# Moving the dense operand tiles by 64 bytes and the experts' operand tiles by 64 bytes in a two-block transformer kernel

## The chip, the cores and the metric

The kernel runs on one core of one Trainium2 chip. The metric is the device time of one execution in microseconds. The kernel before takes 1743.59 us, the median of three runs (1742.76 to 1747.4).

## The reference, cut to what matters

256 tokens of width 1024 pass through two blocks, all in float32. The first has a gated convolution branch, an attention with latent queries and keys, and a feed-forward part with a short convolution. The second has a pooling and convolution mixer, a gated feed-forward part, a sliding-window attention, and a mixture of 8 experts with two experts for each token:

```python
def swiglu(h, w_gate, w_up, w_down):
    return (jax.nn.silu(h @ w_gate) * (h @ w_up)) @ w_down

def moe_swiglu(h, w_router, w_gate, w_up, w_down):      # 8 experts, hidden width 3584
    ...
    for e in range(N_EXPERTS):
        out = out + combine[..., e:e + 1] * swiglu(h, w_gate[e], w_up[e], w_down[e])
```

Every large product is `h @ w` with h of 256 rows, or the 128 gathered rows of one expert. The weights are read once from HBM, in some 450 pieces of 1 MB.

## The kernel before, in words

**Products in three parts.** A float32 product is made of three products in the type fp32r. Each weight and each operand is split into a high part (rounded to fp32r) and a low part (the rest). The helper `three` (lines 771 to 773) issues high times high, high times low and low times high into the same PSUM bank. A name such as `psum<-ah,whi` in the profile gives the output, then the operand that streams through TensorE (the moving operand, here `ah`), then the one that is loaded into it beforehand (the stationary operand, here a 128x128 piece of `whi`).

**Weights.** They arrive in granules of 128 x 2048 numbers (1 MB) in the six slots of `wraw`. ScalarE writes a granule's high part to `whi` (three slots), VectorE its low part to `wlo` (three slots): lines 1261 and 1593, and line 1660. The SP queue loads the next granule when VectorE is through with the slot. ScalarE's split waits until TensorE has used the slot of `whi` that it overwrites.

**Dense stages.** Here the weights are stationary, and an operand of 128 x 256 numbers moves; one granule holds 16 pieces and makes 48 matmuls. Which operand tiles move depends on the stage. `ah` and `al` (high and low, eight chunks of 256 columns) hold the normalised input: of the first projection, both up projections, the mixer's input and the second attention's queries, keys and values. `fh`/`fl` serve the two down projections, `mh`/`ml` the products `w_out` and `mix_out`, `oh`/`ol` and `lnh`/`lnl` the outputs of attention and of the convolution branch (`oh` in this profile stands for both attentions' tiles).

**Experts.** The loop runs over 8 experts with 42 granules each. Here the operand is stationary: a 128x128 piece of `xgh`/`xgl` (the gathered inputs) for the gate and up products, or of `ath`/`atl` (the activations) for the down product. 512 columns of `whi` or `wlo` move. Four transposes (line 1184) stand between groups of these.

**Placement.** The helper `place(name, shape, dtype, at)` puts a tile into SBUF. Without `at` tiles follow one another from the start address, each size rounded up to 64 bytes; with `at` a tile lies at that offset from the address `region`, which follows the last tile of the first kind. All tiles of the first kind before `ah` (`wraw`, `whi`, `wlo`) have sizes that are multiples of 8 KB. Call their start address B modulo 128. Then `ah` and `al` start at B too. After them come `xres` and `sq` (8 KB each), five tiles of 1 KB, `par` (496 numbers, 1984 bytes), `con` (rounded 1408), `ones` (512), `st` (128), `gfg` and `nsk` (64 each), `rgain` (256), `rtm` and `flag` (64 each). Of these only sizes that are odd multiples of 64 matter modulo 128: `par` (31 times 64) and the four of 64 bytes. So `region` starts at B + 64 modulo 128. The tiles `fh`, `fl`, `mh`, `ml`, `lnh`, `lnl`, `oh`, `ol`, `oh2`, `ol2` and, in the experts, `xgh`, `xgl`, `ath`, `atl` are all at multiples of 128 from `region`. So are `last`, `ylh` and `yll`, with which the last matmuls of the kernel (lines 1241 and 1242) pick out the last expert's rows: `last` is stationary, 512 columns of `ylh` or `yll` move, and these operands are fp32r too.

Of the kernel before, what the change touches and what calls it, by code (L numbers as in the profile page):

```python
# [15 lines left out]
P = 128  # L16
T = 256
D = 1024
KD = D // P
# [8 lines left out]
NE = 8  # L28
# [253 lines left out]
def program(nc, wall, x_d, params_d, consts_d, pos_d, onehot_d, relb_d, poolw_d, recip_d, fgain_d,  # L282
            mgain_d, scratch, rows_in, rows_out, out_d):
    f32, f32r, i32 = mybir.dt.float32, mybir.dt.float32r, mybir.dt.int32
# [4 lines left out]
    with ctx:  # L289
        top = [(nc.sbuf_base + 63) // 64 * 64]  # L290

        def place(name, shape, dt, at=None):

            size = (int(np.prod(shape[1:])) * 4 + 63) // 64 * 64
            off = top[0] if at is None else region + at
            if at is None:
                top[0] += size
            assert at is None or at + size <= region_size, name
            return nc.alloc_sbuf_tensor_at(name, shape, dt, offset=off)
# [5 lines left out]
        wraw = place("wraw", [P, NW, GW], f32)  # L305
        whi = place("whi", [P, NS, GW], f32r)
        wlo = place("wlo", [P, NS, GW], f32r)
        ah_at = top[0]
        ah = place("ah", [P, KD, T], f32r)
        al = place("al", [P, KD, T], f32r)  # L310
        xres = place("xres", [P, KD, T], f32)
# [8 lines left out]
        par = place("par", [P, NPARAM], f32)  # L320
        con = place("con", [P, NCONST], f32)
        ones = place("ones", [P, P], f32)
        st = place("st", [P, 2, 16], f32)
        gfg = place("gfg", [P, KD], f32)
        nsk = place("nsk", [P, NH2], f32)
        rgain = place("rgain", [P, KD, NE], f32)
        rtm = place("rtm", [P, 2], f32)
        flag = place("flag", [P, 1], i32)
        region = top[0]
        region_size = nc.sbuf_usable_end - 64 - region  # L330
        KB = 1024
# [62 lines left out]

        zeros = place("zeros", [P, D], f32, 20 * KB)

        xgh = place("xgh", [P, KD, P], f32r, 0)
        xgl = place("xgl", [P, KD, P], f32r, 4 * KB)
        ath = place("ath", [P, 2, 4, P], f32r, 8 * KB)
        atl = place("atl", [P, 2, 4, P], f32r, 12 * KB)  # L400
        htm = place("htm", [P, 2, D], f32, 16 * KB)
        xtm = place("xtm", [P, 2, D], f32, 24 * KB + 128)
        mgain = place("mgain", [P, D + P], f32, 64 * KB + 128)
        hrow = place("hrow", [P, 2, DW], f32, 56 * KB)
# [23 lines left out]
        xgt = place("xgt", [P, D], f32, 48 * KB)  # L428
        ysb = place("ysb", [P, D], f32, 52 * KB)
        yrow1 = place("yrow1", [P, 2, D], f32, 56 * KB)  # L430
        yrow2 = place("yrow2", [P, 2, D], f32, 16 * KB)
        outb = place("outb", [P, 2, D], f32, 0)
        ylh = place("ylh", [P, D], f32r, 48 * KB)
        yll = place("yll", [P, D], f32r, 8 * KB)
# [1973 lines left out]
```

## Time and profile before

| | us |
|---|---|
| median of the runs | 1743.59 |
| the profiled execution | 1746.71 |
| its span, first to last instruction | 1744.9 |
| granted TensorE clock, mean share of full speed | 0.991 |

The profiled execution is 3.1 us above the median and inside the range of the runs; 1.8 us of it lie outside the span. The experts' loop runs from about 768 to 1728 us of the span, the dense stages lie before it. In the profile, TensorE's matmul records overlap, since matmuls are pipelined: the start of one to the start of the next is the pace, while the duration of one is longer and has a modelled end. Weight loads are a row of their own (PEld).

### The profile page before, as it was taken

What the parts mean: (1) busy time and instruction counts of PE and PEld (TensorE: products, weight loads), DVE (VectorE), ACT (ScalarE), POOL (GpSimd) and SP (SyncE); (2) the same over time, 40 slices, a digit from 0 to 9 for tenths busy, and PEclk for the clock granted to TensorE, in tenths of its full rate; (3) what the DMA queues carried; (4) which work ended last, traced back from release to release, by engine and by line L of the source; (5) the groups of instructions that cost most, each with busy time, mean ns of one, the idle gap of its engine ahead of it and who ended that gap; (6) DMA issues with size and microseconds to landing.
All of it is one profiled execution on the core that took longest, in us unless ns stands there. A gap on an engine that the chain in (4) does not pass through costs nothing.

```text
span 1744.9 us, 26269 instructions
## 1 busy us (share of the span) xinstructions
PE 1709.2 (98%) x10136; PEld 1514.7 (87%) x10136; DVE 1418.2 (81%) x1392; ACT 1125.2 (64%) x1132; POOL 189.8 (11%) x167
## 2 busy tenths in 40 slices
PE   8999999999999999899999999999999999999997
PEld 8989999999999999887888888888888888888885
DVE  6996788857866657677888888888888888888888
ACT  5325577653544445566777777777777777777775
POOL 6000354412400011020000000000000000000200
PEclk9999999999999999999999999999999999999998
DMA  8335599894555555159999999999999999999993
GB/s 320 128 121 193 151 234 337 320 254 173 180 183 194 180 198 161 73 197 408 397 368 381 382 377 380 364 385 387 359 390 380 369 380 380 379 383 352 398 422 154
DMA packets 75614, 513.50 MB, mean 294 GB/s; under 512 B 8368, under 2 KB 8848, under 8 KB 17424
## 3 DMA queue, kind: packets, MB, share of 16 engines
q1 hardware_dynamic: 68832, 487.13, 73.9%
q0 software_dynamic: 6560, 25.31, 5.4%
q8 instruction: 52, 0.85, 0.2%
q14 instruction: 26, 0.21, 0.0%
q10 hardware_dynamic: 144, 0.00, 0.0%
HBM read 488.27 MB, written 24.14 MB: 294 GB/s over the span
## 4 chain that ended last, share of the span: by engine, by line
PE 86%; DVE 7%; ACT 2%; issue 1%; DMA 1%; POOL 1%; DVEq 0%; SPq 0%; POOLq 0%; ACTq 0%
PE psum L771 27%; PE psum L773 26%; PE psum L772 26%; PE psum L824 3%; DVE wlo L1660 2%; PE psum L1184 1%; DVE acc L1744 1%; DMA wraw<-weights 1%; ACT whi L1261 1%; PE psum L1049 0%; PE psum L1152 0%; PE psum L905 0%; PE psum L926 0%; ACT whi L1593 0%; DMA par<-params 0%
## 5 line engine op out<-in xcount | busy, mean ns | idle before, releaser
L1660 DVE TENSOR_TENSOR wlo<-wraw,whi 128x2048 fp32r<-128x2048 f32 x445 | 1014.5, 2280 | 198.8 <-ACT whi L1593 115.6
L1593 ACT ACTIVATE whi<-wraw 128x2048 fp32r<-128x2048 f32 x336 | 644.6, 1919 | 234.2 <-PE psum L773 225.5
L771 PE MATMUL psum<-whi,xgh 128*128 128x512 f32 x896 | 357.8, 399 | 2.9 <-DVE wlo L1660 2.0
L773 PE MATMUL psum<-whi,xgl 128*128 128x512 f32 x896 | 351.1, 392 | 0.0
L772 PE MATMUL psum<-wlo,xgh 128*128 128x512 f32 x896 | 350.0, 391 | 0.0
L771 PE MATMUL psum<-ah,whi 128*128 128x256 f32 x1048 | 299.9, 286 | 4.4 <-DVE u L1750 3.9
L772 PE MATMUL psum<-al,whi 128*128 128x256 f32 x1048 | 297.2, 284 | 0.0
L773 PE MATMUL psum<-ah,wlo 128*128 128x256 f32 x1048 | 297.1, 284 | 0.0
L1261 ACT ACTIVATE whi<-wraw 128x2048 fp32r<-128x2048 f32 x104 | 198.5, 1910 | 123.5 <-PE psum L773 119.6
L771 PEld LDWEIGHTS psum<-ah,whi 128*128 128x128 f32 x1048 | 201.7, 192 | 5.9 <-DVE u L1750 4.5
L773 PEld LDWEIGHTS psum<-whi,xgl 128*128 128x128 f32 x896 | 168.6, 188 | 39.3
L772 PEld LDWEIGHTS psum<-al,whi 128*128 128x128 f32 x1048 | 201.8, 193 | 0.3
L773 PEld LDWEIGHTS psum<-ah,wlo 128*128 128x128 f32 x1048 | 201.8, 193 | 0.0
L771 PEld LDWEIGHTS psum<-whi,xgh 128*128 128x128 f32 x896 | 168.8, 188 | 37.2 <-DVE wlo L1660 2.4
L772 PEld LDWEIGHTS psum<-wlo,xgh 128*128 128x128 f32 x896 | 168.9, 188 | 34.7
L771 PE MATMUL psum<-whi,ath 128*128 128x512 f32 x448 | 177.8, 397 | 0.0
L773 PE MATMUL psum<-whi,atl 128*128 128x512 f32 x448 | 175.3, 391 | 0.0
L772 PE MATMUL psum<-wlo,ath 128*128 128x512 f32 x448 | 174.7, 390 | 0.0
L755 POOL DMA_INDIRECT yrow<-expert_outs,idx x4 | 9.6, 2398 | 867.2 <-SPq L560 866.3
L773 PEld LDWEIGHTS psum<-whi,atl 128*128 128x128 f32 x448 | 84.1, 188 | 19.5
L772 PEld LDWEIGHTS psum<-wlo,ath 128*128 128x128 f32 x448 | 84.2, 188 | 17.6
L771 PEld LDWEIGHTS psum<-whi,ath 128*128 128x128 f32 x448 | 84.2, 188 | 17.3 <-DVE wlo L1660 0.3
(349 smaller groups left out, 2234.6 us busy)
## 6 DMA issues: line engine op xcount, KB each, us to landing
wraw<-weights SPq DMA_DIRECT2D x453, 1024.0 KB, 5.1
expert_rows<-zeros POOLq DMA_DIRECT2D x1, 8704.0 KB
expert_outs<-zeros POOLq DMA_DIRECT2D x1, 4608.0 KB
expert_outs<-ysb SPq DMA_DIRECT2D x8, 512.0 KB, 6.5
xgt<-expert_rows SPq DMA_DIRECT2D x8, 512.0 KB, 6.0
bias_rows<-ttab POOLq DMA_DIRECT2D x1, 3072.0 KB, 37.2
btab<-bias_rows POOLq DMA_DIRECT2D x4, 384.0 KB, 8.1
xres<-x SPq DMA_DIRECT2D x1, 1024.0 KB, 5.0
```

The costliest lines, as they stand in the source:

```text
L755: pool.indirect_dma_start(out=dst[:, t, :], out_offset=None, in_=rows_out, in_offset=bass.IndirectOffsetOnAxis(ap=idx[:, i:i + 1], axis=0) ...
L771: nc.tensor.matmul(out, lh, rh, start=start, stop=False)
L772: nc.tensor.matmul(out, lh, rl, start=False, stop=False)
L773: return nc.tensor.matmul(out, ll, rh, start=False, stop=stop)
L824: mm = nc.tensor.matmul(jb(n), wraw[:, g % NW, off:off + P], x[:, k, :], start=(k == 0), stop=(k == PLAN.jobs[n][-1][2]))
L1184: mm = nc.tensor.transpose(bank[6][:, i * P:(i + 1) * P], act_[:, i * P:(i + 1) * P], ident)
L1261: sc.activation(whi[:, i % NS, :], wraw[:, g % NW, :], ACT.Copy).then_inc(hi_done, 1)
L1593: sc.activation(whi[:, (GS + j) % NS, :], wraw[:, g % NW, :], ACT.Copy).then_inc(hi_done, 1)
L1660: return ve.tensor_tensor(dst, value, hi.bitcast(f32), SUB)
L1744: ve.scalar_tensor_tensor(acc[:, c, :], u[:, c, tap:tap + T], pcol("conv_dw_w", 4 * tap + c), acc[:, c, :], MUL, ADD).then_inc(conv_step, 1)
```

## The change

Three small tiles are placed ahead of `ah` where before they came after `ones`. They take 128 + 256 + 64 = 448 bytes, so `ah`, `al`, and all from there to `ones` start 448 bytes later, which is 64 bytes modulo 128. The sum of all sizes is the same, so `region` does not move. Five tiles of the experts' part, and `yrow2`, get 64 bytes more in their offset from `region`. No instruction is added, removed or put in another place.

Modulo 128, before: `ah`/`al` at B as the weights, `xgh`/`xgl`/`ath`/`atl` at B + 64. After: `ah`/`al` at B + 64, `xgh`/`xgl`/`ath`/`atl` at B as the weights. All others named above stay at B + 64. `xres`, `sq`, `rstd` and their like move with `ah` to B + 64.

```diff
         wlo = place("wlo", [P, NS, GW], f32r)
-        ah_at = top[0]
+        st = place("st", [P, 2, 16], f32)
+        rgain = place("rgain", [P, KD, NE], f32)
+        flag = place("flag", [P, 1], i32)
         ah = place("ah", [P, KD, T], f32r)
         al = place("al", [P, KD, T], f32r)
...
         ones = place("ones", [P, P], f32)
-        st = place("st", [P, 2, 16], f32)
         gfg = place("gfg", [P, KD], f32)
         nsk = place("nsk", [P, NH2], f32)
-        rgain = place("rgain", [P, KD, NE], f32)
         rtm = place("rtm", [P, 2], f32)
-        flag = place("flag", [P, 1], i32)
...
-        xgh = place("xgh", [P, KD, P], f32r, 0)
-        xgl = place("xgl", [P, KD, P], f32r, 4 * KB)
-        ath = place("ath", [P, 2, 4, P], f32r, 8 * KB)
-        atl = place("atl", [P, 2, 4, P], f32r, 12 * KB)
-        htm = place("htm", [P, 2, D], f32, 16 * KB)
+        xgh = place("xgh", [P, KD, P], f32r, 64)
+        xgl = place("xgl", [P, KD, P], f32r, 4 * KB + 64)
+        ath = place("ath", [P, 2, 4, P], f32r, 8 * KB + 64)
+        atl = place("atl", [P, 2, 4, P], f32r, 12 * KB + 64)
+        htm = place("htm", [P, 2, D], f32, 16 * KB + 64)
...
-        yrow2 = place("yrow2", [P, 2, D], f32, 16 * KB)
+        yrow2 = place("yrow2", [P, 2, D], f32, 16 * KB + 64)
```

## Rows read from the trace of the kernel before

**Rows 1.** The page: busy time by engine, and the chain that ended last, by line.

```profile
PE 1709.2 (98%) x10136; PEld 1514.7 (87%) x10136; DVE 1418.2 (81%) x1392; ACT 1125.2 (64%) x1132; POOL 189.8 (11%) x167
...
PE psum L771 27%; PE psum L773 26%; PE psum L772 26%; PE psum L824 3%; DVE wlo L1660 2%; PE psum L1184 1%; DVE acc L1744 1%; DMA wraw<-weights 1%; ACT whi L1261 1%; PE psum L1049 0%; PE psum L1152 0%; PE psum L905 0%; PE psum L926 0%; ACT whi L1593 0%; DMA par<-params 0%
```

**Rows 2.** The page's costliest groups: busy us, mean ns of one, idle before.

```profile
L1660 DVE TENSOR_TENSOR wlo<-wraw,whi 128x2048 fp32r<-128x2048 f32 x445 | 1014.5, 2280 | 198.8 <-ACT whi L1593 115.6
L771 PE MATMUL psum<-whi,xgh 128*128 128x512 f32 x896 | 357.8, 399 | 2.9 <-DVE wlo L1660 2.0
L771 PE MATMUL psum<-ah,whi 128*128 128x256 f32 x1048 | 299.9, 286 | 4.4 <-DVE u L1750 3.9
L773 PEld LDWEIGHTS psum<-ah,wlo 128*128 128x128 f32 x1048 | 201.8, 193 | 0.0
L771 PE MATMUL psum<-whi,ath 128*128 128x512 f32 x448 | 177.8, 397 | 0.0
```

**Rows 3.** Line 771's matmuls counted in stretches of stages in which `ah` moves.

```profile
219.00:330.00 111.00, 87.04 (x308) 1.00 0.97 312
480.00:590.00 110.00, 86.52 (x306) 1.00 0.53 187
```

**Rows 4.** The same, stretches in which `fh` moves.

```profile
345.00:395.00 50.00, 40.59 (x148) 1.00 0.99 257
600.00:656.00 56.00, 45.44 (x166) 1.00 0.55 200
```

**Rows 5.** The same, stretches in which `mh` moves.

```profile
192.00:207.00 15.00, 12.16 (x45) 1.00 0.49 184
451.00:469.00 18.00, 14.31 (x52) 1.00 0.50 173
```

**Rows 6.** Groups of one stretch, 598 to 657 us: weight loads beside `fh`.

```profile
L773 PEld LDWEIGHTS psum<-fh,wlo 128*128 128x128 f32 x175 | 32.9, 188 | 0.0
```

**Rows 7.** Timeline (start us, us), TensorE in the steady run of an expert.

```profile
1301.31 0.39 PE L771 MATMUL psum<-whi,xgh 128*128 128x512 f32 x1
...
1303.37 0.39 PE L771 MATMUL psum<-whi,xgh 128*128 128x512 f32 x1
```

**Rows 8.** Timeline, the first two matmuls of an expert's group after transposes.

```profile
1300.53 0.48 PE L771 MATMUL psum<-whi,xgh 128*128 128x512 f32 x1
...
1300.85 0.40 PE L772 MATMUL psum<-wlo,xgh 128*128 128x512 f32 x1
```

**Rows 9.** Timeline, the end: matmuls of `ylh`, `yll` with `last` stationary.

```profile
1732.72 0.47 PE L1241 MATMUL psum<-ylh,last 128*128 128x512 f32 x1 [3.53 <-DVE yll L1660]
...
1733.03 0.40 PE L1242 MATMUL psum<-yll,last 128*128 128x512 f32 x1
...
1733.96 0.63 PE L1241 MATMUL psum<-ylh,last 128*128 128x512 f32 x1
...
1735.24 0.63 PE L1242 MATMUL psum<-yll,last 128*128 128x512 f32 x1
```

**Rows 10.** Durations (ns, min/median/max) of both kinds' first matmuls.

```profile
L771 PE MATMUL psum<-whi,xgh x1: 481/481/481, 1300.5 to 1300.5; 128*128 128x512 f32 x1
...
L1241 PE MATMUL psum<-ylh,last x2: 467/472/478, 1732.7 to 1733.3; 128*128 128x512 f32 x2
```

**Rows 11.** Clock after 1733.6: us, busy PE, PEld, DVE, ACT, POOL, PEclk, DMA share, GB/s.

```profile
1733.60:1745.00 11.40, 2.27 (x6) 1.27 (x4) 7.55 (x10) 2.60 (x6) 0.00 (x0) 0.50 0.23 93
```

**Rows 12.** The same columns, 120 us of the experts.

```profile
900.00:1020.00 120.00, 120.00 (x544) 98.69 (x543) 105.80 (x59) 89.82 (x62) 0.00 (x0) 1.00 0.97 377
```

**Rows 13.** The page's slices of 43.6 us: GB/s moved.

```profile
GB/s 320 128 121 193 151 234 337 320 254 173 180 183 194 180 198 161 73 197 408 397 368 381 382 377 380 364 385 387 359 390 380 369 380 380 379 383 352 398 422 154
```

**Rows 14.** Waits, 800 to 1728 us: us in total, times, longest.

```profile
ACT whi L1593 <- PE psum L773: 223.1, 309, 0.8
...
ACT whi L1593 <- DMA wraw<-weights: 2.1, 2, 1.6
```

**Rows 15.** VectorE groups that write `al` and `ml`.

```profile
L1702 DVE SCALAR_TENSOR_TENSOR al<-xres,gfg,ah 128x256 fp32r<-128x256 f32 x8 | 3.8, 477 | 0.2 <-ACT ah L1279 0.2
...
L1992 DVE SCALAR_TENSOR_TENSOR ml<-psum,par,mh 128x256 fp32r<-128x256 f32 x4 | 1.9, 478 | 1.2 <-ACT mh L1443 1.2
```

**Rows 16.** From issue to landing of the four gathers into `yrow1` and `yrow2`.

```profile
DMA to landing us min/median/max: 9.6/11.5/12.8
```

## Prediction

> **What bounds the kernel now.** I read the page first: TensorE is busy for 98% of the span, and in the chain that ended last the three lines of `three` hold 79%, VectorE's `wlo` 2% [rows 1]. So the pace of the fp32r matmuls is the time. Of those with an offset that the change touches there are 3 x 1048 = 3144 with `ah` or `al` moving, 3 x 896 with `xgh`/`xgl` and 3 x 448 with `ath`/`atl` stationary, 4032 in the experts; their idle before is a few us [rows 2]. Durations overlap and have modelled ends, so I take paces from counts in a stretch and from starts.
>
> With `ah` moving, line 771 stands 308 times in 111 us and 306 times in 110 us: one in 360 ns, and since it is every third matmul, 120.0 ns for one [rows 3]. With `fh` moving it stands 148 times in 50 us and 166 in 56 us: 338, at the edges 340 ns, 113.3 ns for one [rows 4]. Same shape, same clock, same three lines, same length of stretch. The DMA share does not explain it: each kind has a stretch at 0.97 or more and one near 0.54, with no difference. What differs is the address: `ah` lies in step with the weights modulo 128, `fh` 64 bytes off. `mh` is 64 off too, and shows 45 in 15 us (340 ns) in one product and 52 in 18 us, 51 intervals, 353 ns or 117.7 each, in the other [rows 5]. So 64 off has two paces, 113.3 and 117.7, and in step has one, 120.0. A weight load lasts 193 ns beside `ah` and 188 beside `fh`, and in both there is no idle before it [rows 2, 6]. I read this as two streams that read SBUF at once, the load of the next weights and the moving operand, and that get in each other's way more when they start at the same place modulo 128.
>
> **The dense part.** The change gives `ah` and `al` the relation that `fh` and `mh` have. 120.0 - 113.3 = 6.7 ns at the better pace, 2.3 ns at the other. Of the steady time 64 off in this trace (two down products of 61 and 60 us, some 45 us of `mla_out`, `conv_out`, `w_out`, 24 us of the mixer's product) only the last and a few us more run at 117.7, a sixth. So one matmul gains 5/6 x 6.7 + 1/6 x 2.3 = 6.0 ns, and 3144 gain 18.9 us. In the second attention some 240 of them stand between steps of a softmax chain, where an earlier end is partly waited away: 1.4 us off, and 0.5 for the first matmuls after waits. Taken: 17 us. Bounds: 3144 x 2.3 = 7 us and 3144 x 6.7 = 21 us. Nothing comes late in its place: VectorE's 2.28 us for `wlo` [rows 2] stand against 48 x 113.3 = 5.4 us of matmuls for a granule.
>
> **The experts' part.** No row shows an expert's matmul in step. 64 off, nine matmuls from 1301.31 to 1303.37 take 2.06 us, 229 ns each [rows 7]. The array alone would need less: at the half clock [rows 11] the last matmuls, 512 columns of fp32r, go 1.28 us for three, 427 ns each, 213 at the full clock [rows 9]. So 16 ns of each 229 are something else, and half the time no weight load runs beside. The only fp32r matmuls with 512 columns and in-step operands are those last ones (`last`, `ylh`, `yll` all start at multiples of 128 from `region`). Compare like with like, the first after a pause, with the load of the second operand beside it: 0.32 us to the next for the expert's, 0.31 for `ylh`'s [rows 8, 9]; durations 481 ns against 467 and 478 [rows 10]. The differences are 3 to 14 ns, in favour of in step. Two instances only, and in another phase than the steady run, but they are the nearest rows, and they point against what the dense stages would make one expect. Why the sign could differ: in the dense stages the load is without a pause and sets the pace (no idle before it); here it has some 110 ns of slack and the moving operand sets it, so what counts is which of the two gives way.
>
> Price: I take 6.7 ns, the one step between states that the dense rows show and near the middle of 3 and 14. 4032 x 6.7 = 27 us. Bounds: a gain of all that lies above 213, 16 ns, is 64 us; a loss of 6.7 ns as in the dense stages is 27 us, and of twice that, since twice as many columns move, 54 us.
>
> Is anything next to late? VectorE is busy 105.8 of 120 us in the experts [rows 12]; with 3% less time, 116.5 us, that is 91%, tight but no bound. The traffic is 377 GB/s at a DMA share of 0.97 [rows 12] and would be 389; slices with 398, 408 and 422 stand on the page [rows 13], and ScalarE waits 223 us for TensorE and 2.1 us for the weights' DMA [rows 14]. I cost this at nothing; without that cover the experts keep their 960 us and the 27 us are gone.
>
> **The small edits** go together. VectorE takes 477 ns for `al` with all operands on the weights' side and 478 ns for `ml` with its two on the region's side [rows 15], so `xres`, `rstd` and the statistics tiles cost nothing by moving. Bounds: 40 such instructions at 1 ns, nothing. `yrow2` becomes the target of a gather that starts 64 bytes off; the gathers land in 9.6 to 12.8 us [rows 16], started at 1645 to 1653 us and first read at 1729, so even twice that is covered by 60 us of experts. `htm` serves 32 matmuls once.
>
> **The sum.** 17 + 27 = 44 us off the profiled execution's 1746.7 gives 1702.7, and off its span 1744.9 gives 1701. It stood 3.1 us above the median, so in medians 1743.6 - 44 = 1700 us.
>
> **A rule against it.** Both streams' paces in rows 3 and 4 speak of interference inside TensorE's reading. The Trainium skill (SBUF — State Buffer, Who interferes with whom) gives TensorE two independent read ports and says that it never waits on anyone; and TensorE: Matmul & The Clock Gate (Part 2, Step-by-step) says that loading the next weights takes no bandwidth from the running matmul. By that rule 64 bytes change nothing. This case's trace disagrees: 120.0 against 113.3 ns.
>
> **Rivals.**
>
> 1. The experts do not care: their load has 110 ns of slack, and what it loses is hidden. For: load and matmul compete only in the first half of 229 ns, and rows 8 to 10 are two instances of a first matmul. Against: the constant 16 ns that something costs. Only the dense part acts: 1743.6 - 17 = 1727 us.
>
> 2. Slower: in step costs the experts what it costs the dense stages. The price is at each weight load beside a moving operand, 6.7 ns, and there are 4032 in the experts against 3144 that are relieved. For: the only steady rows of both offsets say that in step is worse. Against: rows 8 to 10. -17 + 27 = +10: 1754 us. It decides against the change from 17000 / 4032 = 4.2 ns for one matmul upwards; at the doubled price it is 1781.
>
> 3. The experts' matmuls do get faster, but the weights' stream or VectorE stops them a third of the way: 17 + 9 = 26 us off, 1718 us. For: 0.97 and 91%. Against: the waits in rows 14.
>
> 4. The 113 and 120 ns come from something else in those stages than the offset (where the streams began, which instructions run beside), and nothing moves: 1743.6 us. Against: three tiles in five stretches at 64 off, none of them at 120, and no stretch of `ah` below it. This is also where the rule above would end.
>
> **How the numbers follow.** Forecast, both parts gain: 0.45, on its own 1687 to 1714 (dense 12 to 20, experts 18 to 37). Rival 1: 0.23, 1722 to 1735. Rival 2: 0.19, 1746 to 1770. Rival 3: 0.08. Rival 4: 0.05. The likeliest case is the forecast, 1700. A range that leaves 2 in 10 out goes from 1686, below which lie the larger gains of the experts up to 64 us, to 1755, above which lies the upper half of rival 2. A measurement of this kernel tells a change from none at about 0.3%, 5 us. Faster by more than that are the forecast, rivals 1 and 3, and a trace of the others: 0.77. Within it: rival 4 and the edge of rival 2: 0.06. Slower: 0.17.
>
> **What would show it.** In the changed kernel's stretches of `ah`, line 771 would stand some 325 times in 110 us (340 ns) or 312 times (353) instead of 306; weight loads beside `ah` would last 188 ns. In the experts nine matmuls would take 2.00 us instead of 2.06, and the loop 27 us less. If nine take 2.06, it is rival 1; 2.12, rival 2; if their pace between waits is 222 but idle time of TensorE before line 771 or 1184 appears, with `wlo` or the weights' DMA as its cause, rival 3. The forecast is wrong if the experts' matmul is over 226 ns, or if `ah` stays at 120.

## The result, and the profile after

The changed kernel takes 1731.25 us, the median of seven runs (1727.87 to 1736.04), against 1743.59 for the kernel before, run beside it (seven runs, 1740.54 to 1747.4). The ratio is 0.993, with an interval from 0.9916 to 0.9944. So it is faster by 12.3 us where 44 were forecast: short of the forecast, and inside the range. The profiled execution took 1730.13 us, its span is 1728.3 and the mean clock 0.994 (before: 1746.71, 1744.9 and 0.991). Line numbers are one lower than before: `three` is now L770 to L772, `wlo` L1659.

The page says the same of the bound as [rows 1]: TensorE is at 98% of a shorter span, and `three` holds 78% of the chain that ended last.

```profile
PE 1687.0 (98%) x10136; PEld 1497.7 (87%) x10136; DVE 1416.8 (82%) x1392; ACT 1125.9 (65%) x1132; POOL 188.9 (11%) x167
PE psum L770 26%; PE psum L772 26%; PE psum L771 26%; DVE wlo L1659 3%; PE psum L823 3%; DMA wraw<-weights 2%; PE psum L1183 1%; DVE acc L1743 1%; ACT whi L1260 1%; PE psum L1048 0%; PE psum L1151 0%; PE psum L904 0%; PE psum L925 0%; ACT whi L1592 0%; PE psum L1047 0%
```

The dense stages first, by the busy time by stretches of TensorE's instructions of line 770 alone (us, busy and count, granted clock, DMA share, GB/s). Every third matmul is of this line, so the count gives the pace of three. The first two stretches have `ah` moving (first and second up projection), the next two `fh`, the last two `mh`.

```profile
240.00:320.00 80.00, 64.96 (x236) 1.00 1.01 318
480.00:580.00 100.00, 79.53 (x284) 1.00 0.53 190
345.00:380.00 35.00, 28.41 (x104) 1.00 0.99 219
590.00:640.00 50.00, 39.73 (x143) 1.00 0.54 190
190.00:203.00 13.00, 10.57 (x39) 1.00 0.56 188
442.00:458.00 16.00, 12.99 (x48) 1.00 0.47 151
```

80 us / 236 = 339 ns, and 100 us / 284 = 352: `ah` has left its 360 ns [rows 3] for the two paces that `fh` and `mh` showed, 113.3 and 117.7 ns for one matmul. But see the fourth line. `fh` in the second down product was not touched by the change and stood at 340 ns [rows 4]; now it goes at 50 / 143 = 350, in starts 353. In the trace it belongs to one unbroken run with the second up projection before it: 1583 matmuls from 467.7 us on, all at the pace of 353. And `mh` in its second product was at 353 [rows 5] and is now at 16 / 48 = 333, at the edges 340. So the same place gives one pace or the other in different executions. The weight loads beside `ah` went from 193 ns [rows 2] to the 188 of [rows 6] where the pace is 340, as the groups of the weight load's row from 240 to 320 us show. Where it is 353, from 480 to 580 us, the loads of one line of the three last 192 ns and those of the other two 188:

```profile
L772 PEld LDWEIGHTS psum<-ah,wlo 128*128 128x128 f32 x236 | 44.3, 188 | 0.0
```
```profile
L772 PEld LDWEIGHTS psum<-ah,wlo 128*128 128x128 f32 x283 | 54.3, 192 | 0.0
L771 PEld LDWEIGHTS psum<-al,whi 128*128 128x128 f32 x284 | 53.3, 188 | 0.0
```

In the kernel before all three lines have 192 beside `ah` (490 to 590 us). So there the load's time follows the pace: three long loads at 360, one at 353, none at 340.

Then the experts. The timeline of TensorE (start, duration) shows nine matmuls from 1299.39 to 1301.43 us, 2.04 us or 226.7 ns each, against 2.06 us or 229 [rows 7]. The four transposes at 1302.80 open a new group, and from its first matmul to the second it is 0.32 us, as before [rows 8]. By the starts in the traces the median of this step over some 54 groups went from 320 to 314 ns, near the 6.7 of the price. But the kernel with the experts' tiles of before (e1 below) shows 313, so this step does not follow the offset, and it says nothing of the steady pace.

```profile
1299.39 0.39 PE L770 MATMUL psum<-whi,xgh 128*128 128x512 f32 x1
...
1301.43 0.39 PE L770 MATMUL psum<-whi,xgh 128*128 128x512 f32 x1
...
1302.80 0.60 PE L1183 MATMUL psum<-con,act__135 128*128 128x128 f32 x4
1303.15 0.48 PE L770 MATMUL psum<-whi,xgh 128*128 128x512 f32 x1
1303.47 0.40 PE L771 MATMUL psum<-wlo,xgh 128*128 128x512 f32 x1
1303.70 0.40 PE L772 MATMUL psum<-whi,xgl 128*128 128x512 f32 x1
1303.93 0.40 PE L770 MATMUL psum<-whi,xgh 128*128 128x512 f32 x1
```

Is anything else late now? The waits from 790 to 1710 us (us, times, longest) say no: ScalarE still waits 217 us for TensorE (223 before) and 1.8 us for the weights' DMA (2.1 before, [rows 14]).

```profile
ACT whi L1592 <- PE psum L772: 217.4, 310, 0.8
ACT whi L1592 <- DMA wraw<-weights: 1.8, 1, 1.8
```

Where the 16.6 us of span went, from the starts of all matmuls in both traces. The first expert matmul starts at 756.5 us instead of 767.8: 11.3 us are of the dense part. The experts' loop, first to last start, takes 953.9 instead of 959.6: 5.7 us; behind it 0.4 us are lost. The clean measure of the experts' pace is the mean start-to-start time of adjacent expert matmuls, those of 300 ns and more (waits and first ones) left out: 229.05 ns before, 227.42 after, 1.63 ns x 4032 = 6.6 us.

The 11.3 us are not the offset's alone. TensorE's whole row up to the first expert matmul, of the kernel before, of e2 below (the dense part's addresses as before) and of the changed kernel:

```profile
0.00:767.80 767.80, 747.04 (x5802) 0.99 0.60 199
```
```profile
0.00:761.30 761.30, 740.61 (x5803) 1.00 0.60 200
```
```profile
0.00:756.50 756.50, 730.87 (x5803) 1.00 0.61 202
```

Before its first expert matmul the trace of before has 17.1 us at a granted clock of 0.50 (1.2 GHz instead of 2.4; the first such stretch, 44.0 to 47.4 us, comes behind a wait of TensorE of 3.08 us for VectorE), e2 has 3.4 and the changed kernel 6.8. Half of such a stretch is lost, so 5.1 of the 11.3 us are the clock's, and 6.2 are left. The busy time, the clock's share taken off, fell by 16.2 - 5.1 = 11 us; the idle time rose from 20.8 (20.7 in e2) to 25.6 us. So the faster matmuls gave 11 us, and 4.8 of these went into longer waits of TensorE, spread over the dense stages that have waits. Over the whole span the mean clocks of 0.991 and 0.994 make 5 of the 16.6 us, which leaves about the 12.3 of the medians.

### The profile page after: what moved, and what is told of

It reads as the page before. It is cut to its first block, busy times and chain, and to the rows that moved or that the text cites. A ratio compares the mean times of both kernels' runs of the same rounds, so it can differ in the third digit from the quotient of the medians.

```text
span 1728.3 us, 26269 instructions
## 1 busy us (share of the span) xinstructions
PE 1687.0 (98%) x10136; PEld 1497.7 (87%) x10136; DVE 1416.8 (82%) x1392; ACT 1125.9 (65%) x1132; POOL 188.9 (11%) x167
## 4 chain that ended last, share of the span: by engine, by line
PE 86%; DVE 8%; ACT 2%; DMA 2%; issue 1%; SPq 0%; DVEq 0%; ACTq 0%
PE psum L770 26%; PE psum L772 26%; PE psum L771 26%; DVE wlo L1659 3%; PE psum L823 3%; DMA wraw<-weights 2%; PE psum L1183 1%; DVE acc L1743 1%; ACT whi L1260 1%; PE psum L1048 0%; PE psum L1151 0%; PE psum L904 0%; PE psum L925 0%; ACT whi L1592 0%; PE psum L1047 0%
## 5 line engine op out<-in xcount | busy, mean ns | idle before, releaser
L1659 DVE TENSOR_TENSOR wlo<-wraw,whi 128x2048 fp32r<-128x2048 f32 x445 | 1014.5, 2280 | 194.0 <-ACT whi L1592 110.0
L1592 ACT ACTIVATE whi<-wraw 128x2048 fp32r<-128x2048 f32 x336 | 645.1, 1920 | 228.2 <-PE psum L772 219.7
L770 PE MATMUL psum<-whi,xgh 128*128 128x512 f32 x896 | 354.7, 396 | 3.5 <-DVE wlo L1659 2.6
L772 PE MATMUL psum<-whi,xgl 128*128 128x512 f32 x896 | 350.4, 391 | 0.0
L770 PE MATMUL psum<-ah,whi 128*128 128x256 f32 x1048 | 294.6, 281 | 3.8 <-DVE u L1749 1.9
L771 PE MATMUL psum<-al,whi 128*128 128x256 f32 x1048 | 291.7, 278 | 1.2 <-issue 1.2
L772 PE MATMUL psum<-ah,wlo 128*128 128x256 f32 x1048 | 291.6, 278 | 0.0
L770 PEld LDWEIGHTS psum<-ah,whi 128*128 128x128 f32 x1048 | 196.9, 188 | 5.6 <-DVE u L1749 2.5
L770 PEld LDWEIGHTS psum<-whi,xgh 128*128 128x128 f32 x896 | 168.7, 188 | 37.8 <-DVE wlo L1659 3.0
L772 PEld LDWEIGHTS psum<-whi,xgl 128*128 128x128 f32 x896 | 168.4, 188 | 36.1
L772 PEld LDWEIGHTS psum<-ah,wlo 128*128 128x128 f32 x1048 | 198.3, 189 | 0.8 <-issue 0.8
L771 PEld LDWEIGHTS psum<-al,whi 128*128 128x128 f32 x1048 | 197.0, 188 | 1.1 <-issue 0.8
L770 PE MATMUL psum<-whi,ath 128*128 128x512 f32 x448 | 176.0, 393 | 0.1
L772 PE MATMUL psum<-whi,atl 128*128 128x512 f32 x448 | 174.6, 390 | 0.0
L770 PEld LDWEIGHTS psum<-whi,ath 128*128 128x128 f32 x448 | 84.1, 188 | 17.7 <-DVE wlo L1659 0.5
L772 PEld LDWEIGHTS psum<-whi,atl 128*128 128x128 f32 x448 | 84.1, 188 | 17.6
```

The costliest lines, as they stand in the source:

```text
L770: nc.tensor.matmul(out, lh, rh, start=start, stop=False)
L771: nc.tensor.matmul(out, lh, rl, start=False, stop=False)
L772: return nc.tensor.matmul(out, ll, rh, start=False, stop=stop)
L1592: sc.activation(whi[:, (GS + j) % NS, :], wraw[:, g % NW, :], ACT.Copy).then_inc(hi_done, 1)
L1659: return ve.tensor_tensor(dst, value, hi.bitcast(f32), SUB)
```

## The experiments

Ratios are to the kernel before, run beside it on the same chip, with a 95% interval. Paces are the time from one line-770 matmul to the next, three matmuls, in ns.

### Each part alone

The first kernel has the changed placement ahead of `ah` and the experts' tiles of before; the second the reverse.

```diff
 # e1_dense_only, against the changed kernel
-        xgh = place("xgh", [P, KD, P], f32r, 64)
+        xgh = place("xgh", [P, KD, P], f32r, 0)
 ... (xgl, ath, atl, htm, yrow2 alike)
 # e2_experts_only, against the changed kernel
-        st, rgain, flag ahead of ah
+        st, rgain, flag behind ones, as before
```

> Only the dense half of the change (three small tiles ahead of ah; ah, al and the tiles behind them 64 bytes later); the experts' tiles as in the kernel before. Theory A (each part's pace is set by its own operand's offset from the weights modulo 128, and the parts add): three ah matmuls take 340 or 353 ns instead of 360, three expert matmuls stay at 687; the first expert matmul comes 8 to 14 us earlier and the time is 7 to 13 us under the kernel before. Theory B (the gain of the changed kernel comes mostly from the experts' part, the dense stages only trade paces): under 4 us.

> Only the experts' half of the change (xgh, xgl, ath, atl, htm, yrow2 64 bytes later); the dense part as in the kernel before. Theory A: three expert matmuls take 680 ns instead of 687, 2.3 ns for one, at most 9 us for 4032; some of it goes into slower groups (691 to 697 ns after transposes, more idle before wlo), so the time is 3 to 9 us under the kernel before. Theory B (the weights' DMA or VectorE holds the experts' loop, 0.97 of the DMA engines' time): the pace inside a group falls and idle time takes it back, 0 to 2 us.

Measured beside 1741.5 us of the kernel before: dense alone 1733.76 us, ratio 0.9959 (0.9946 to 0.9973), by the ratio 7.1 us off and by the medians 7.7; experts alone 1734.5, ratio 0.9963 (0.9949 to 0.9977), by the ratio 6.4 us off and by the medians 7.0. The sum of the ratios, 13.5 us, is the whole change's 12.3 within the intervals: no sign that the parts touch each other. All TensorE records from 900 to 1500 us, by stretches, of the kernel before, dense alone, experts alone, and the changed kernel:

```profile
900.00:1500.00 600.00, 600.00 (x2714) 1.00 0.97 377
```
```profile
900.00:1500.00 600.00, 600.00 (x2718) 1.00 0.97 378
```
```profile
900.00:1500.00 600.00, 600.00 (x2732) 1.00 0.98 380
```
```profile
900.00:1500.00 600.00, 600.00 (x2732) 1.00 0.97 381
```

Both kernels with the experts' tiles in step have 2732 records, 0.5 to 0.7% more than the two without. The mean pace of an expert's matmul is 228.90 ns in dense alone and 227.40 in experts alone. So the experts do gain from lying in step, the opposite of the dense stages, and by a quarter to a third of the price forecast. In the steady stretches three take 680 instead of 687 ns, 2.2 ns for one. But that holds for 1032 of the 1279 groups of three that I could follow in the changed kernel. Behind most groups of transposes the in-step run goes 235, 233, 236, 224, 231, 236, 228, 233, 231 ns after its first step before it settles at 226.7, where 64 off goes 235, 232, 231 and then 229 in the mean. That start gives back 2.2 - 1.6 = 0.6 ns of the mean.

In dense alone only 178 groups of three with `ah` ran at 340 ns and 818 at 353; in the changed kernel's trace it was 558 and 438. That goes the way of its smaller dense gain (first expert matmul at 762.5, 6.0 us behind the changed kernel's). Such splits of one trace need the clock as well. In experts alone, with `ah` at 360 throughout, the first expert matmul came 6.5 us earlier than in the kernel before: it had 3.4 us at the half clock against 17.1, which is worth 6.9. The medians of the kernels are the firmer measure.

### What the offset has to be

The diff and the forecast speak of 64 bytes modulo 128. If that were the rule, +64 would do as well as the place that the change uses, and other offsets would lie between. e3 puts `ah` at 32 and `fh` and `xgh` at 96 modulo 128, e4 `ah` at 96 and `fh` and `ath` at 0.

```diff
 # e3_offsets_32_96 (e4_offsets_96_0: 96 and 32), against the kernel before
+        top[0] += 32
         ah = place("ah", [P, KD, T], f32r)
         al = place("al", [P, KD, T], f32r)
+        top[0] += 96
 ... fh, fl, mh, ml, xgh, xgl, ath, atl, htm, yrow2 by 0 to 128 bytes to the offsets below
```

> Other offsets from the weights modulo 128: ah and al 32 (xres and all behind it keep their place modulo 128), fh and fl 96, mh and ml 32, xgh and xgl 96, ath and atl 32. Theory A1 (only whether bit 6 of the address is the same counts, so 32 is like 0 and 96 like 64): ah 360 ns for three, fh 340 or 353, mh 360, experts 687 with xgh, 680 with ath. Theory A2 (the distance in time until the moving operand meets the load counts, so each offset has a pace of its own): paces other than 340, 353, 360 and 680, 687. Theory C (the moved statistics tiles give the gain, not ah): ah 360.

> Offsets from the weights modulo 128: ah and al 96 (the tiles behind keep their place modulo 128), fh, fl, mh, ml 0 instead of 64, xgh and xgl 64 as before, ath and atl 0. Theory A: fh and mh go from 340 or 353 to 360 ns for three (about 1.1 us more for each 176 of 3 matmuls in a down product, some 5 to 8 us in all), experts 687 with xgh and 680 with ath. A1: ah 340 or 353. A2: ah has a pace of its own. Theory D (the stage sets the pace, not the offset): fh and mh stay at 340 and 353, ah at 360.

Measured: 1759.36 us, ratio 1.0102 (1.0087 to 1.0117), and 1761.79, ratio 1.0119 (1.0103 to 1.0134). Both are slower than the kernel before. The gap around `ah` adds up to 128 bytes and moved `region` by as much. By a rule modulo 128 that is nothing. But in e4 `xgh` lies 64 off modulo 128 as before and went from 687 to 697 to 703. So 128 bytes more made it another place. (`oh`, moved by the same 128 bytes, stood at 353 in all but 4 of its groups of three; as the two paces change from one execution to the next at one place, that alone shows little.) Worked out from the sizes in the section on placement: the small tiles sum to 4544 bytes and the five of 1 KB, `xres` and `sq` and `ah`/`al` to multiples of 512, so `region` is at 448 modulo 512 from the weights, which is -64. The next four kernels ask for the sign and the period: +64; -64 and 0 moved by 256; and what is left of the steps of 32.

```diff
 # e5_plus_64, against the kernel before; e6: 448 and 320, e7: 416 and 96, e8: 384 and 0
+        top[0] += 64
         ah, al
+        top[0] += 448
 ... (the operand tiles to the offsets below)
-        q2 = place("q2", [P, KD, T], f32, 48 * KB)
+        q2 = place("q2", [P, KD, T], f32, 47 * KB)
 ... (btab, k2, v2, s2 alike, 1 KB down, to make room)
```

> Offsets from the weights are counted modulo 512 from here on: the kernel before has ah at 0 and all other operand tiles at 448 (64 bytes short of the next 512), the changed one ah at 448 and the experts' tiles at 0. Here: ah and al at +64, fh and fl at 0, mh and ml at +64, oh and lnh at 448 as before (control), all experts' tiles at +64. Theory M128 (only the offset modulo 128 counts, as the change is worded; 64 and 448 are the same): ah 340 or 353 ns for three, mh 340 or 353, fh 360, experts 687. Theory M512 (the offset counts with its sign, to a modulus of 256 or more): ah and mh 353 only, never 340, as lnh and oh had it where they were moved to +64 in the third experiment; experts 697 to 703; fh at 0: 360 by both.

> ah and al at 448 (as in the changed kernel, with only the tiles behind them elsewhere), fh, oh, lnh at 192, mh at 256, xgh and xgl at 192, ath and atl at 256. M128: 192 and 448 are the same: fh, oh, lnh 340 or 353, xgh 687; 256 is 0: mh 360, ath 680. Modulus 256: the same numbers. Modulus 512: fh and lnh, mh, xgh, ath show paces other than at 448 and 0. In all: ah 340 or 353.

> ah at 416 (96 short), fh, mh and xgh at 480 (32 short), ath at 32, oh and lnh at 448 (control, 340 or 353). M128: ah like 32, where the third experiment had 346 to 355; fh, mh like 96 (357 to 364), xgh like 96 (700 to 707), ath like 32. M256 or more: a pace of its own for each; if the interference falls off with distance on the short side, ah at 416 is at or under 340, and xgh at 480 lies between 680 and 687.

> ah at 384, fh, oh, lnh and xgh at 320, mh at 416, ath at 384. M128: ah 360 and ath 680 (like 0), fh, lnh 340 or 353 and xgh 687 (like 64). M256: ah and ath like 128 (351 to 360; 691 to 706), fh, lnh and xgh like 64 (353; 697 to 703). M512: paces of their own.

One run each, beside 1743.29 us of the kernel before: 1760.02, 1734.73, 1758.87 and 1756.86. The operand tiles of all these kernels, by their start minus the weights' start modulo 256, with the time of three matmuls (in brackets where it was seen):

| modulo 256 | dense, 256 columns move | experts, 512 columns move |
|---|---|---|
| 0 | 360 (before, e2: `ah`; e6: `mh`) | 680 (after, e2: all; e6: `ath`) |
| 32 | 346 to 355 (e3: `ah`) | 695 to 702 (e7: `ath`) |
| 64 | 352 to 355 (e5: `ah`), 353 (e8: `fh`), and 340 in one or two short runs of each | 697 to 704 (e4, e5, e8: `xgh`) |
| 96 | 356 to 365 (e4: `ah`, e3: `fh`) | 699 to 707 (e3: `xgh`) |
| 128 | 351 to 361 (e8: `ah`, e4: `fh`) | 690 to 706 (e4, e8: `ath`) |
| 160 | 350 to 361 (e7: `ah`, e3: `mh`) | 700, a few 710 (e3: `ath`) |
| 192, that is -64 | 340 or 353 (before: `fh`, after, e6) | 687 (before, e1; e6: `xgh`) |
| 224 | 351 to 360 (e7: `fh`, `mh`) | 697 to 704 (e7: `xgh`) |

How such a pace is read, by stretches for one line of `three`: 490 to 590 us (`ah` moves) and 605 to 650 us (`fh` moves), of the kernel before (line 771):

```profile
490.00:590.00 100.00, 78.62 (x278) 1.00 0.53 189
605.00:650.00 45.00, 36.55 (x133) 1.00 0.57 207
```

of e5, where `ah` is at +64 and `fh` in step:

```profile
490.00:590.00 100.00, 79.12 (x284) 1.00 0.52 184
605.00:650.00 45.00, 35.45 (x126) 1.00 0.53 188
```

and of e6, where both are 256 bytes further than in the changed kernel:

```profile
605.00:650.00 45.00, 36.56 (x134) 1.00 0.55 201
```

`fh` in step stands 126 times in 45 us (357 ns, in starts 360) where at -64 it stood 133 times (338): the tile that the change never touched takes up the pace of `ah` when it is put where `ah` was. This is the test of rival 4 from the other side. At -64 plus 256 it is 134 again. +64 is not free of the faster pace: in e8 `fh` went through a first run of 59 matmuls at 340 and through the 512 behind it at 353, and e5 has two short runs of `ah` at 340. The first run of e8 and most of the second, line 772:

```profile
332.00:338.50 6.50, 5.30 (x20) 1.00 0.61 226
339.60:395.00 55.40, 43.97 (x157) 1.00 0.94 244
```

In the experts, e5 and e6 from 900 to 1500 us:

```profile
900.00:1500.00 600.00, 600.00 (x2669) 1.00 0.96 371
```
```profile
900.00:1500.00 600.00, 600.00 (x2718) 1.00 0.97 378
```

At +64 the mean pace is 233.3 ns, 4.3 above the kernel before, x 4032 = 17 us, about e5's whole loss of 16.7; of its dense stages `ah` gains and `fh` loses. At -64 plus 256 for the gate and up products it is 228.61. So the period is 256 bytes, and in the experts the sign counts: 687 ns at -64, 697 to 704 at +64, in three kernels. In the dense stages the sign shows only in how seldom +64 had the faster pace. The weights stay in their place in all kernels here, so nothing tells an offset from the weights from a tile's own address modulo 256; "offset" stands for both. Of the eight places in the table 0 and -64 are the two best for the experts, 0 ahead, and -64 is best for the dense stages when it runs at 340 (at 353 it is no better than 32), where 0 is among the worst. The kernel before used these two the wrong way round for `ah` and for the experts, and the change gave each part its best one. The five kernels with most tiles elsewhere (e3, e4, e5, e7, e8) lost 0.8 to 1.2%.

### What picks 340 or 353

In all traces an unbroken run of dense matmuls at -64 holds one of the two paces from a dozen matmuls after its start to its end, never a mixture. Something at the start picks it. These kernels put short float32 matmuls of known size (8, 128 or 256 columns into an unused bank) between two jobs.

```diff
 # e9_breaks, against the changed kernel
+            def breaks(widths):
+                for w_ in widths:
+                    mov_ = con if w_ > P else ones
+                    nc.tensor.matmul(bank[5][:, 0:w_], ones[:], mov_[:, 0:w_], start=True, stop=True)
             for i in range(2, 2 * NF):
                 job(AT["up1"] + i, ah, al)
+                if i % 4 == 1:
+                    breaks((8,))
 ... (down1: (256,) after each but the last; up2: (128,) after each fourth; down2: (8, 8) after each but the last)
```

> The changed kernel with short float32 matmuls (results unused) that break the streams: 8 columns after every 4th product tile of the first up stage (11 streams of 96 matmuls instead of one of 1008), 256 columns after each tile of the first down stage, 128 columns after every 4th tile of the second up stage, two of 8 columns after each tile of the second down stage. Theory E (the pace of 340 or 353 ns for three is drawn when a stream begins and then held): within a stream one pace, from stream to stream either, so each of the four stages shows both, and the second up stage, held at 353 throughout in the changed kernel's trace, has some streams at 340. Theory S (the stage, what runs beside it on ScalarE and VectorE or the slot of the weights sets it): the second up and down stages stay at 353, the first ones at 340 after the first break. Price of the breaks: 36 of them at 0.2 to 0.5 us, 8 to 15 us.

> The changed kernel once more. Theory E: the shares of 340 and 353 differ from its first trace (558 against 438 of the ah triples) although nothing differs in the program, and the time with them: 1029 triples at 13 ns is 13 us between all at one and all at the other, so runs spread by several us. Theory S: the same stages hold the same paces. The median is 8 to 14 us under the kernel before by both.

Measured: with breaks 1743.06 us, ratio 0.9974 (0.9959 to 0.9988); the changed kernel again 1735.88, ratio 0.9931 (0.9916 to 0.9945), the same ratio as in the first comparison, beside 1747.51. A break costs 0.23 us with 8 columns, 0.24 with 128, and 0.43 to 0.48 with 256 columns or with two of 8. A single one of 8 columns found `ah` at 340 ns ten times and left it there ten times. One of 128 found 353 once, and behind it 340, and then left 340 nine times. One of 256 went both ways, seven cases. Two of 8 swapped the pace at each of seven. The stretches between four of these in e9 (line 770, `fh`) have 19, 20, 19 and 20 records in 6.50 us. A count of that size says only that they alternate; by the starts three take 353, 340, 353 and 340 ns.

```profile
604.00:610.50 6.50, 5.20 (x19) 1.00 0.61 216
612.00:618.50 6.50, 5.26 (x20) 1.00 0.50 171
620.00:626.50 6.50, 5.17 (x19) 1.00 0.67 237
628.00:634.50 6.50, 5.28 (x20) 1.00 0.45 161
```

Hence a version: nine single breaks of 8 columns in the changed kernel, each early in a run, so that a run at 353 gets one more draw and, if 340 is kept, nothing is lost but 0.23 us. Beside it the kernel before with the same nine, since a pause might act in another way, and the changed kernel for a third time.

```diff
 # e11_changed_short against the changed kernel, e12_before_short against the one before
+            def short():
+                nc.tensor.matmul(bank[5][:, 0:8], ones[:], ones[:, 0:8], start=True, stop=True)
             for i in range(2, 2 * NF):
                 job(AT["up1"] + i, ah, al)
+                if i in (2, 14, 28):
+                    short()
 ... (one in the attention's output product, one each in down1, mix, mix_out, two in up2)
```

> The changed kernel with nine float32 matmuls of 8 columns (results unused), one shortly after the start of each long dense stream, since in the run with breaks all ten streams behind such a one went at 340 ns. Theory E8 (this break always leads to 340, and the pace is held to the end of the stream): ah, fh and mh streams behind one show 340 alone; against the changed kernel's two traces some 470 ah and 190 fh triples go from 353 to 340, 8 us, less nine breaks of 0.2 us: 5 to 7 us under the changed kernel beside it, 17 to 20 under the kernel before. Theory R (340 behind it was luck or came of what stood before it): the streams are drawn anew, no gain, 2 us lost.

> The kernel before with the same nine short matmuls. ah in step goes back to 360 ns behind each; only the fh and mh streams that were at 353 (some 60 matmuls of down1, 165 of mix_out) can gain, 1 us, against 2 us for the breaks: 0 to 3 us over the kernel before by E8, 2 to 4 by R.

> The changed kernel beside the two with short matmuls, to compare on one chip: 8 to 14 us under the kernel before; a share of 340 among the ah triples that is again another one (0.54 and 0.47 so far).

Measured beside 1741.78 us of the kernel before: e11 1722.69, ratio 0.9889 (0.9876 to 0.9902); e12 1743.53, ratio 1.001 (1.0001 to 1.0019); e13 1727.77, ratio 0.9917 (0.9904 to 0.993). In the kernel before the nine cost 1.7 us, and `ah` stays at 360 ns behind each: a pause alone brings nothing at offset 0. In the changed kernel they bring 5.1 us net. Four stretches of line 770 in e11, two in each up projection:

```profile
250.00:285.00 35.00, 28.41 (x104) 1.00 1.01 318
290.00:320.00 30.00, 24.37 (x89) 1.00 1.01 405
480.00:525.00 45.00, 36.51 (x133) 1.00 0.56 201
531.00:580.00 49.00, 39.78 (x145) 1.00 0.55 194
```

and e13 over the same two projections:

```profile
240.00:320.00 80.00, 63.65 (x227) 1.00 1.00 344
480.00:580.00 100.00, 79.53 (x284) 1.00 0.53 188
```

35 / 104 = 337, 30 / 89 = 337, 45 / 133 = 338 and 49 / 145 = 338 ns: e11 is at 340 in all four. e13 is at 352 in both. Of the groups of three with `ah` 193 are at 353 in e11 and 729 in e13; with the other tiles it is 437 against 1013: 576 x 13.3 ns = 7.7 us, less 9 x 0.23 = 2.1, is 5.6, near the 5.1 between the medians. The profiled pair itself differs by 2.7 us only, and its first expert matmuls by 3.6 (756.9 against 760.5); before them e11 has 13.7 us at the half clock and e13 6.8, which hides 3.4 us. One break in e11's timeline, with the pace of 340 on both sides of it (286.23 to 286.57 is three matmuls; 286.70 to 287.13 is three with the first one's 0.20):

```profile
286.23 0.28 PE L770 MATMUL psum<-ah,whi 128*128 128x256 f32 x1
...
286.57 0.28 PE L950 MATMUL psum<-ones 128*128 128x8 f32 x2
286.70 0.36 PE L770 MATMUL psum<-ah,whi 128*128 128x256 f32 x1
...
287.13 0.28 PE L770 MATMUL psum<-ah,whi 128*128 128x256 f32 x1
287.25 0.28 PE L771 MATMUL psum<-al,whi 128*128 128x256 f32 x1
287.36 0.28 PE L772 MATMUL psum<-ah,wlo 128*128 128x256 f32 x1
287.47 0.28 PE L770 MATMUL psum<-ah,whi 128*128 128x256 f32 x1
```

The expectation of e11, that this break always leads to 340, is refuted. In e9, e11 and the tiles at -64 of e12 sixteen single 8-column breaks found 340: behind fifteen it was 340 again, behind one (e12, `oh`, 159.9 us) 353. Six found 353: four led to 340, and two (e11, 213.8 and 336.6 us) did not. That is far from an even draw, and six cases are few. The intervals of e11 and e13 touch at 0.990; with the paces and the clocks of the two traces, which account for the difference, I hold the gain for real, but its size rests on five runs each.

## Why the prediction was off: its steps

**The mechanism: right for the dense stages, in its main point.** The place of the operand tile sets TensorE's pace. `ah` went from 120.0 ns to 113.3 and 117.7, its loads from 193 to 188 ns, and e5 and e6 show `fh` and `mh` at 120.0 once they lie in step. Rival 4, that the paces come from something else, is refuted, and so is the rule that was weighed against the change. The Trainium skill (SBUF — State Buffer, Who interferes with whom) has TensorE never waiting on anyone. This case's runs disagree: here it pays 6.7 ns for a matmul by an address. The period was wrong: 256 bytes and not 128. So the step of 448 bytes was -64, and +64 is another place: in e5 it cost 4.3 ns for an expert's matmul.

**The dense term, 17 us: the mechanism right, the size off.** That part alone measured 7.1 us (7.7 by the medians), and the profiled pair, the clock taken off, 6.2; the 11.3 of the pair as it stands are nearer to 17 by the luck of its clocks. Two steps failed. The first is the share of the slower pace: one sixth, read from where the kernel before happened to show it. In the changed kernel's trace it is 438 of 996, 44%, and in the other two traces of it 51% and 73%. With 44% it is 558 x 20 + 438 x 6.5 ns = 14.0 us, less 2.3 for the second down product, which fell to 353 in this execution, plus 0.7 for `mix_out`, which rose: 12.4 us, against the 11 that the busy time shows. I had read the two paces as belonging to tiles and stages; they belong to runs of matmuls and change from one execution to the next. The four stretches of `fh` and `mh` in one trace (the prediction counts five of three tiles, its rows show four of two) could not show this, but the fact that `mh` had both, in one trace, at one address, should have kept the share open between 0 and 1. The second step is the overlap with waits: 1.9 us were taken off for the softmax chain and first matmuls, and TensorE's idle time before the experts rose by 4.8. The bounds of 7 and 21 us hold for the part alone, at their lower end.

**The experts' term, 27 us: the sign right, the size off, and this is most of the error.** The step that failed is the price of 6.7 ns. It measured 1.63 in the mean (6.6 us) and 2.2 to 2.3 in the steady run (9 us). At 226.7 ns the prediction's own sign of being wrong, over 226, came true. The price was taken from first matmuls after a pause [rows 8 to 10], which turned out to say nothing: that first step takes 314 ns after the change and 313 in e1, where the experts' tiles did not move, and in the nine steps behind it in step loses 15 ns against 64 off. That the sign came out right is luck, then. The likeness that I took for comparison (512 columns, in step) hid that phase and operand roles matter as much. The dense rows held a smaller step as well, 117.7 to 113.3 and 117.7 to 120.0, and the last of these, 2.3 ns, happens to be the size. The slack of the load was no help either: the prediction has no load running half the time, while its [rows 12] have the weight loads busy for 98.69 of 120 us, and in the experts they last 188 ns in both kernels, though the pace changed. No row priced this term. With its ends at -54 and +64 us and no row inside, the honest value was near zero, which is rival 1.

**Rivals.** Rival 1, the experts do not care, gave 1727 us and came nearest to the time, but not by its mechanism: they do care, by a quarter of the price, and its 17 us of dense gain were too much. Rival 2, the experts slower, is refuted by e2, 0.9963 with nothing but their tiles moved. Of its idea one thing is left: in step is worse in the first nine steps behind the first matmul after transposes. Rival 3, another bound, is refuted for the experts by the waits: nothing new stands before TensorE, and in the steady stretches it goes at 226.7 ns with no idle time before it.

**The small edits: right.** ScalarE's 1920 ns for `whi` and VectorE's 2280 for `wlo` are as before, and e1 and e2 add up to the whole.

What stays open: why 0 and -64 are the good places and with opposite ranks in the two parts, and whether what counts is the offset from the weights at all or the tile's own address, since no run moved the weights. That the load of the next weights and the moving operand meet in SBUF is argued from the loads' 192 and 188 ns in the dense stages; in the experts the loads last 188 ns at 0, at -64 and at +64 alike, while the pace goes from 226.7 to 233, so there this sign is missing. No run here separates it from other ways in which an address could matter. What picks the pace at the start of a run is open too, and whether it is a fair draw: the second up projection went at 353 ns in all four traces with the changed dense placement and without a short matmul in it (after, e1, e10, e13), but in e6, where `ah` lies at -64 too, it went at 340. Line 772 there, from 490 to 590 us:

```profile
490.00:590.00 100.00, 81.34 (x295) 1.00 0.55 196
```

## What to carry to other kernels

Where a stream of matmuls sets the time, compare its pace from counts or starts between stages of the same shape: a few ns for one matmul that go with a tile's name and not with the traffic can be an address, and moving tiles by tens of bytes is a cheap experiment, to be tried per stage and over the whole period, since the best place of one stage is the worst of another. Price a steady pace only by steady rows: a comparison of first instructions after a pause gave neither its size nor, but by luck, its sign. Before a part of a trace is compared with another, take off what the granted clock did in each, and look whether the time gained came back as waits. Where one trace shows two paces at one address, take the share of each as unknown.

## What the runs showed that was not expected

- The place of an fp32r matmul's operand tile counts modulo 256 bytes: three experts' matmuls take 680 ns at 0 from the weights, 687 at -64 and 690 to 710, mostly about 700, elsewhere; three dense ones 360 at 0, 340 or 353 at -64, and 346 to 365 elsewhere (at +64 in short runs 340 as well). +64, the mirror image, for the experts' tiles, `ah` and `mh`, with `fh` in step, costs the kernel 1% (1760.02 against 1743.29 us).
- At -64 a run of dense matmuls locks into 340 or 353 ns for three and holds it over hundreds of matmuls (1583 in one run, the changed kernel's second up and down products).
- A single float32 matmul of 8 columns between two such matmuls costs 0.23 us, left 340 as it was in 15 of 16 cases and turned 353 into 340 in four of six. Two of them swapped the pace in 7 of 7. With nine such breaks the changed kernel ran in 1722.69 us, the best of all kernels here, 19.1 us under the kernel before beside it.
